# A two-block transformer kernel on one core: expert gates made by one-hot products in PSUM, or scattered into a DRAM table

## The reference, cut to what matters

```python
def peer(xn, peer_w_q, peer_sub_keys, peer_u, peer_v):
    qh = (xt @ peer_w_q).reshape(T, PEER_HEADS, 2, PEER_HALF)
    sub = jnp.einsum("thpc,hpnc->thpn", qh, peer_sub_keys)
    v1, i1 = lax.top_k(sub[:, :, 0], PEER_TOPK)      # 16 of 128
    v2, i2 = lax.top_k(sub[:, :, 1], PEER_TOPK)
    vals, cidx = lax.top_k(v1[..., :, None] + v2[..., None, :], PEER_TOPK)
    experts = e1 * N_KEYS + e2
    gates = jax.nn.softmax(vals, axis=-1)
    # y[token] = sum over its 128 (head, k): gelu(x . u[expert]) * gate * v[expert]
```

## Time and profile before

| | |
|---|---|
| three runs | 3204.29, 3204.08, 3206.46 us |
| profiled execution | span 3203.0 us |
| TensorE matmul busy | 3185.0 us, 99% |
| VectorE busy | 2226.0 us, 69% |
| ScalarE busy | 1555.5 us, 49% |
| GpSimd busy | 13.7 us, 0% |
| DMA | 610.61 MB, 191 GB/s; SyncE's queue 60.0% of 16 engines |
| granted TensorE clock | 0.9 or more in every slice |

### The profile page before, as it was taken

The page is one execution under the profiler, slowest core; times in us unless marked ns, Lnnn a source line. Parts: engine busy times, 40 slices in busy tenths (PEclk is TensorE's granted clock), DMA queues, the critical chain, the costliest instruction groups (busy, mean ns, idle before and its releaser), DMA issues.

```text
span 3203.0 us, 42378 instructions
## 1 busy us (share of the span) xinstructions
PE 3185.0 (99%) x17362; PEld 2707.6 (85%) x17362; DVE 2226.0 (69%) x3055; ACT 1555.5 (49%) x1998; POOL 13.7 (0%) x29
## 2 busy tenths in 40 slices
PE   9999999999999999999999999999999999999999
PEld 8888888888888888887888888888888788888887
DVE  6775556677577567766568997766687787865564
ACT  4564444555355455546544555455443344444353
POOL 0000000000000000000000000000000000000000
PEclk9999999999999999999999999999999999999999
DMA  7456665656665666653555666666666665556665
GB/s 252 154 162 218 211 211 180 210 191 191 191 190 190 193 188 192 205 170 111 190 154 171 217 216 189 188 183 224 190 190 212 203 200 173 188 184 192 194 184 171
DMA packets 175825, 610.61 MB, mean 191 GB/s; under 512 B 19201, under 2 KB 27553, under 8 KB 174736
## 3 DMA queue, kind: packets, MB, share of 16 engines
q1 hardware_dynamic: 173648, 599.93, 60.0%
q0 software_dynamic: 1984, 7.99, 0.8%
HBM read 597.36 MB, written 10.49 MB: 190 GB/s over the span
## 4 chain that ended last, share of the span: by engine, by line
PE 97%; DVE 2%; ACT 1%; issue 0%; DMA 0%; SPq 0%; ACTq 0%; DVEq 0%
PE PS L1194 29%; PE PS L1211 16%; PE PS L1213 16%; PE PS L1212 16%; PE PS L1191 15%; PE PS L1414 1%; PE PS L1427 1%; PE PS L1293 1%; DVE LO L1749 0%; PE PS L1247 0%; PE PS L1326 0%; ACT UN L1506 0%; ACT HI L1436 0%; PE PS L1305 0%; PE PS L1223 0%
## 5 line engine op out<-in xcount | busy, mean ns | idle before, releaser
L1749 DVE TENSOR_TENSOR LO<-RAW,HI 128x1024 fp32r<-128x1024 f32 (+1 forms) x1096 | 1325.1, 1218 | 698.0 <-ACT HI L1436 694.7
L1436 ACT ACTIVATE HI<-RAW 128x1024 fp32r<-128x1024 f32 (+1 forms) x1096 | 1148.3, 1054 | 1044.6 <-PE PS L1213 732.5
L1194 PE MATMUL PS<-XX,HI 128*128 128x512 f32 x4032 | 968.4, 391 | 0.0
L1194 PEld LDWEIGHTS PS<-XX,HI 128*128 128x128 f32 x4032 | 739.4, 188 | 145.1 <-issue 2.4
L1211 PE MATMUL PS<-HI,FH 128*128 128x512 f32 x1760 | 692.0, 393 | 1.7 <-DVE LO L1749 1.7
L1213 PE MATMUL PS<-HI,FL 128*128 128x512 f32 x1760 | 685.8, 390 | 0.0
L1212 PE MATMUL PS<-LO,FH 128*128 128x512 f32 x1760 | 684.7, 389 | 0.0
L1191 PEld LDWEIGHTS PS<-XX,LO 128*128 128x128 f32 x4032 | 520.2, 191 | 21.1 <-issue 1.0
L1191 PE MATMUL PS<-XX,LO 128*128 128x256 f32 x4032 | 536.8, 284 | 0.0
L1213 PEld LDWEIGHTS PS<-HI,FL 128*128 128x128 f32 x1760 | 330.3, 188 | 70.1
L1211 PEld LDWEIGHTS PS<-HI,FH 128*128 128x128 f32 x1760 | 330.3, 188 | 69.1 <-DVE LO L1749 2.2
(11 more groups left out here) (286 smaller groups left out, 1667.7 us busy)
## 6 DMA issues: line engine op xcount, KB each, us to landing
RAW<-in_peer_ut SPq DMA_DIRECT2D x256, 512.0 KB, 4.1
RAW<-in_peer_v SPq DMA_DIRECT2D x256, 512.0 KB, 4.2
RAW<-in_ffn_w_up SPq DMA_DIRECT2D x176, 512.0 KB, 4.2
RAW<-in_w_in SPq DMA_DIRECT2D x88, 512.0 KB, 4.3
RAW<-in_ffn_w_down SPq DMA_DIRECT2D x88, 512.0 KB, 4.2
RAW<-in_w_in_c SPq DMA_DIRECT2D x48, 512.0 KB, 3.7
RAW<-in_w_mix_out SPq DMA_DIRECT2D x32, 512.0 KB, 4.0
RAW<-in_w_in_2c SPq DMA_DIRECT2D x32, 512.0 KB, 3.7
```

The lines of the kernel that those rows point to most:

```text
L1194: m = e.matmul(o, hi[:, k, x], XX[:, 4 * u + k, :, :].rearrange("p h s -> p (h s)"), start=first and k == 0, stop=last and k == 3, skip_gr ...
L1436: return e.activation(dst, src, ACT.Copy) if scale is None else e.activation(dst, src, ACT.Copy, scale=scale)
L1749: return e.tensor_tensor(dst, src, hi.bitcast(F32), ALU.subtract)
```

## The change

`gates` becomes a DRAM table of 16384 experts by 256 tokens (16 MB). It is zeroed by 32 DMAs of 512 KB, DRAM to DRAM, issued by SyncE one after each of the first 32 products of the feed-forward up stage of the first block. Each `choose(t, g)` gets a tenth part after one more yield: VectorE computes the table address of each of its 32 gates per token (`address`, two instructions), and GpSimd issues 32 indirect DMAs (`scatter`), each of which adds one float for each of 128 tokens into the table. Before each head's 16 DMAs GpSimd waits until all earlier ones of the same token half have landed, since two heads can name the same expert. There are 256 in all. `gates_in(c, j)` then loads 512 KB of the table, on GpSimd's queue too: those of chunks 1 and 0 right behind the last scatter, the others when their place in SBUF is free. Tables, one-hots, `gates_sum`, `gates_out`, `gates_side`, the DRAM copies and chunks 3 and 4 set aside all go; only chunks 0, 1, 2 are staged (in GM[2], STAGE, UF), and chunks 3 to 7 go up and down in turn. `rate[0]` stays at 0.68 through the three up stages.

```diff
-    order = [("up", c) for c in (3, 4, 0, 1, 2)] + [("down", c) for c in (1, 0, 2, 3, 4)]
-    order += [(d, c) for c in range(5, 8) for d in ("up", "down")]
+    order = [("up", c) for c in range(3)] + [("down", c) for c in (1, 0, 2)]
+    order += [(d, c) for c in range(3, 8) for d in ("up", "down")]
...
                     product(("f", q, i, b), 4)
+                    if zeroed[0] < ZEROS:
+                        emit("zero", zeroed[0])
+                        zeroed[0] += 1
...
         emit("gate", t, g)
+        yield
+        emit("address", t, g)
+        emit("scatter", t, g)
...
+    def first_gates():
+        for c in (1, 0):
+            for j in range(4):
+                emit("gates_in", c, j)
+        yield
+
     background.extend([first_gates(), first_blocks()])
-    for c in (3, 4, 0, 1, 2):
+    for c in range(3):
         up_staged(c)
...
-    background.extend([gates_back(2), multiply_third()])
+    gates_in(2)
+    background.append(multiply_third())
     down(1, then=0)
-    background.append(gates(2, 3))
+    gates_in(4)
     down(0, then=2)
-    beside.append(gates_back(3))
-    down(2, then=3)
-    down(3, then=4)
-    background.extend([pause(4), gates(3, 3)])
-    down(4)
-    for c in range(5, 8):
+    gates_in(5)
+    down(2)
+    gates_in(3)
+    for c in range(3, 8):
+        if c in (4, 5):
+            gates_in(c + 2)
...
+            elif kind == "zero":
+                n, = k
+                e.dma_start(GATES[:, 1024 * n:1024 * n + 1024], a["zeros"]).then_inc(l_zero, 16)
...
+            elif kind == "scatter":
+                t, g = k
+                w.wait_ge(l_zero, 16 * ZEROS)
+                w.wait_ge(s_dve, V("address", t, g))
+                for h in (2 * g, 2 * g + 1):
+                    if h:
+                        w.wait_ge(l_scatter[t], 256 * h)
+                    for i in range(16 * h, 16 * h + 16):
+                        e.indirect_dma_start(a["gates"], bass.IndirectOffsetOnAxis(IDX[:, t, i:i + 1], 0),
+                                             TK[:, t, i:i + 1], None, compute_op=ALU.add).then_inc(l_scatter[t], 16)
+            elif kind == "gates_in":
+                c, j = k
+                if c < 2:
+                    for t in range(2):
+                        w.wait_ge(l_scatter[t], 256 * 8)
+                else:
+                    w.wait_ge(s_dve, {2: V("second_mul", 3), 3: V("split_up", 2, 3), 4: V("third_mul", 3),
+                                      5: V("split_up", 0, 3), 6: V("weigh", 3, 3), 7: V("weigh", 4, 3)}[c])
+                e.dma_start(GM[PLACE[c]][:, 4 * j:4 * j + 4, :].rearrange("p c s -> p (c s)"),
+                            GATES[:, 4096 * c + 1024 * j:4096 * c + 1024 * j + 1024]).then_inc(l_gates[PLACE[c]][j], 16)
...
             elif kind == "first_mul":
                 j, = k
                 w.wait_ge(s_act, A("us_gelu", 0, j))
-                w.wait_ge(s_act, A("gates_out", 31))
+                w.wait_ge(*gates_landed(0, j))
```

More of the change, by code:

```diff
@@ L22 @@
 LOOK = 3
+NKEY = 128
+ZEROS = 32
 CONSTS = {}
@@ L128 @@
     "best": (0, 0, 5), "cand0": (0, 0, 8), "cand1": (0, 0, 6), "pick0": (0, 0, 7), "pick1": (0, 1, 6),
-    "gate": (0, 0, 3), "tables": (2, 0, 13),
-    "onehot": (0, 0, 3), "gates_sum": (1, 0, 0), "gates_out": (0, 3, 0), "gates_side": (1, 0, 2),
-    "us": (0, 1, 1), "us_gelu": (0, 1, 0), "split_aside": (0, 1, 2), "first_mul": (0, 1, 1), "second_mul": (0, 1, 2), "third_mul": (0, 0, 1), "split_up": (0, 1, 1),
+    "gate": (0, 0, 3), "address": (0, 0, 2),
+    "us": (0, 1, 1), "us_gelu": (0, 1, 0), "first_mul": (0, 1, 1), "second_mul": (0, 1, 2), "third_mul": (0, 0, 1), "split_up": (0, 1, 1),
     "x": (0, 1, 1), "gelu": (0, 2, 0), "weigh": (0, 1, 2), "y": (0, 0, 2),
@@ L652, in plan @@
         background.extend(choose(t, g) for t in range(2))
[L654 to L694, removed]
     staged = [[] for _ in range(5)]
@@ L740, in from_chip @@
             yield from pause(2)
[L742 to L749, removed]
     def down(c, then=None):
@@ L753, in down @@
             if g == 3 and then is not None:
-                beside.append((from_aside if then > 2 else from_chip)(then))
+                beside.append(from_chip(then))
             product(("y", c, g), 8)
@@ L760, in plan, with gates_in @@
     rate[0] = 1
-    background.extend([gates_back(2), multiply_third()])
+    def gates_in(c):
+        for j in range(4):
+            emit("gates_in", c, j)
+    gates_in(2)
+    background.append(multiply_third())
     down(1, then=0)
-    background.append(gates(2, 3))
+    gates_in(4)
     down(0, then=2)
-    beside.append(gates_back(3))
-    down(2, then=3)
-    down(3, then=4)
-    background.extend([pause(4), gates(3, 3)])
-    down(4)
-    for c in range(5, 8):
+    gates_in(5)
[4 more added lines that the diff above has]
+            gates_in(c + 2)
         for j in range(4):
@@ L886, in _program @@
     HB = over("HB", [128, 4, S], 32 * K)
[L887 to L895, removed]
+    IDX = at("IDX", [128, 2, NKEY], U32, offset=gb_at + 4 * K)
     BP = at("BP", [128, 2, S], offset=const_at + 4 * CONSTS["mask2"][0])
-    TAB = at("TAB", [128, 2, S], BF16, offset=mask1_at)
-    KEYS2 = at("KEYS2", [128, 128, 2], BF16, offset=mask1_at + K)
     PS = ctx.enter_context(nc.psum_tensor("PS", [128, 4096], F32))
@@ L992, in _program @@
     l_raw = [sem(f"l_raw{i}") for i in range(NRAW)]
[L993 to L996, removed]
+    l_zero = sem("l_zero")
+    l_scatter = [sem(f"l_scatter{t}") for t in range(2)]
+    l_gates = [[sem(f"l_gates{i}_{j}") for j in range(4)] for i in range(3)]
     l_x, l_ident, l_const, l_par, l_small, l_gb, l_gb1, l_bi, l_gb2, l_keys, l_out = [sem("l_" + n) for n in (
@@ L1022, in multiplied, with gates_landed @@
         return (LAST[step] if u is None else FIRST[step] + u) + 1
-    def gates_read(r, blk):
-        return P("gates_side", r, blk) if r else P("gates_sum", blk)
+    GATES_BY_PLACE = {0: (0, 3, 6), 1: (1, 2, 4, 7), 2: (5,)}
+    def gates_landed(c, j):
+        return l_gates[PLACE[c]][j], 16 * GATES_BY_PLACE[PLACE[c]].index(c) + 16
+    GATES = a["gates"].rearrange("(p x) o -> p (x o)", p=128)
     FFN_ENDS = ("res1", 3), ("d", 0, 3), ("d", 1, 3)
@@ L1395, in tensor @@
                     m.then_inc(s_pe, 1)
[L1396 to L1416, removed]
-            elif kind == "gates_side":
-                r, blk = k
-                i = blk % 2
-                w.wait_ge(s_dve, V("onehot", r, blk))
-                for half in range(2):
-                    for s, n in until_free(step, half):
-                        w.wait_ge(s, n)
-                b0 = 2048 + 512 * PLAN.bank[step, 0]
-                for j in range(8):
-                    o = PS[:, b0 + 128 * j:b0 + 128 * j + 96].rearrange("p (i s) -> p i s", i=3)
-                    m = e.matmul(o, OH2[:, i, j // 2, :, j % 2], GOH[:, i, j // 2, :, :, j % 2], start=True,
-                                 stop=True, skip_group_check=True)
-                m.then_inc(s_pe, 1)
     @block.scalar
@@ L1696, in scalar @@
                 e.activation(dd, dd, ACT.Exp).then_inc(s_act, 1)
-            elif kind == "gates_out":
-                blk, = k
-                w.wait_ge(s_pe, P("n2_turn", 3))
-                w.wait_ge(s_dve, V("gate", 1, 3))
-                w.wait_ge(s_pe, P("gates_sum", blk))
-                src = spare(("gates_sum", blk)).rearrange("p (s k) -> p k s", k=64)
-                for i in range(2):
-                    copy(GM[i][:, :, 8 * blk:8 * blk + 8], src[:, 16 * i:16 * i + 16]).then_inc(s_act, 1)
-                if blk >= 2:
-                    w.wait_ge(l_pass[blk % 2], 16 * (blk // 2))
-                copy(PASS[:, blk % 2].rearrange("p i (k s) -> p (i k) s", s=8), src[:, 32:64]).then_inc(s_act, 1)
             elif kind == "us_gelu":
@@ L1726, in scalar @@
                 copy(blocks(FH, j), blocks(GM[2] if c == 0 else GM[0], j)).then_inc(s_act, 1)
-            elif kind == "split_aside":
-                c, j = k
-                w.wait_ge(s_mm, multiplied(("y", c - 1, 3), 2 * j + 1))
-                w.wait_ge(s_dve, V(*step, k=1))
-                copy(blocks(FH, j), HB[:]).then_inc(s_act, 1)
             elif kind == "gelu":
@@ L2063, in vector @@
                 w.wait_ge(s_act, A(*step))
-                w.wait_ge(s_dve, V("weigh", c, j - 1) if j else V("weigh", c - 1, 3) if c > 5 else V("split_aside", 4, 3))
+                w.wait_ge(s_dve, V("weigh", c, j - 1) if j else V("weigh", c - 1, 3) if c > 3 else V("second_mul", 3))
                 e.tensor_tensor(HB[:, 2 * k[2]:2 * k[2] + 2, :], halves(step)[:, :, 0, :], BP[:],
@@ new lines, in vector @@
+            elif kind == "address":
+                t, g = k
+                first, second = (TK[:, t, 128 * n + 32 * g:128 * n + 32 * g + 32] for n in (1, 2))
+                w.wait_ge(l_const, 16)
+                w.wait_ge(s_dve, V("gate", t, g))
```

(11 more changed lines are left out.)

88 lines of the change are left out of this document (8 added, 80 removed).

## The result

The changed kernel takes **3415.17 us** (3414.29 to 3416.14) against 3204.49 us before: a ratio of 1.0658, 95% interval 1.0643 to 1.0673. That is 211 us slower, and outside the range that was given (3167 to 3310).

What follows compares the result with a forecast made beforehand. TensorE, busy for 99% of the span, was taken to bound the kernel. A 58 us gain less a 39 us stall gave 3204.3 - 19 = 3185 us, likeliest 3175 to 3196, 8 in 10 from 3167 to 3310.

Steps and rivals of the forecast that it cites:

- What goes and what moves: TensorE's first and side passes go, 60 us; two chunks moved to the up-and-down part lose 2: 58 us gain.
- The cheap parts: Zeroing DMAs, address instructions on VectorE and gates_in loads for chunks 2 to 7, all taken as hidden: 0 us.
- Spacing of the groups: Time between successive groups of 32 indirect DMAs while choose runs: 37.6 us.
- The last address: VectorE computes it at unit 82 of the 96 staged ones; first_mul follows 4.1 us later.
- The landings: GpSimd's wait in the middle of a group and the landing of the last indirect DMAs: 4.0 us each.
- The formula: TensorE's stall at first_mul: S = P + 7 x max(0, P - 37.6) + 3.3 us, giving 39 us.
- P: GpSimd's time for one group of 32 indirect DMAs, 32c plus the wait in its middle: 36 us.
- S: TensorE's stall at first_mul while the gates go through GpSimd, DRAM and back: 39 us.
- c: GpSimd's time for one indirect DMA in the scatter: 1.0 us, bounded by 0.51 to 0.56 below and 4.5 above.
- Rival A: GpSimd cannot keep pace with groups 37.6 us apart: slower past c = 1.12 us, 3302 us at 1.5; chance 0.25.
- Rival C: VectorE holds GpSimd up during the scatter: c is 1.6 us, S = 182 us, 3328 us; chance 0.08.
- Rival D: The scatter's adds drain slowly, sharing 16 queues with 512 KB weight loads: 3328 us or more; chance 0.08.

Runs made afterwards that it cites:

- the half scatter: Against the changed kernel, leaves out the gates of every second head, 128 indirect DMAs in place of 256: 3186.6 us.
- the added transfers: Against the changed kernel, adds 80 DRAM-to-DRAM transfers of 512 KB by SyncE while VectorE waits at first_mul: 3502.9 us.

## Why the prediction was wrong, step by step

- *What goes and what moves* (60 less 2, so 58 us): 57.6 us by the kernel without a scatter; 3203.0 - (3414.1 - 264.6) = 53.5 us by the changed kernel's own trace, and 56 if the 2.5 us of low clock behind the stall are taken off too. Right to within some 3 us, about what single runs can tell.
- *The cheap parts* at 0: right. 252 units in 700 us in the zeroing stretch in both kernels, and 82 units in 230 us of the `choose` stretch in both.
- *Spacing of the groups*, 37.6 us: measured 37.8. *The last address*, then `first_mul` at once: right.
- *The landings*, 4.0 us each: 12.8/4 = 3.2 us beside weight traffic, 7.1/4 = 1.8 in the stall. The fixed cost of about 2.0 us that the Trainium skill gives in "DMA: Bandwidth & Descriptors", section "Anatomy of one DMA — SWDGE (gpsimd) path", is nearer the second, once the DMA engines were quiet; small either way.
- *The formula*: with P = 65.1, S = 65.1 + 7 x 27.5 + 3.3 = 261 us; TensorE's stall measured 263. Right, and confirmed at 37 us by the half scatter. Two numbers taken from it were worked out wrongly, and neither moves the forecast: at c = 4.5 it gives 924 us and not 1050, and at c = 1.07 a time of 3192 us and not 3196.
- **The step that failed: "To it I add as much again, rounded down, for fetching 128 indices and for the add: c = 1.0 us."** It measured 1.96: 0.96 for an indirect store, 0.58 more for the add, 0.12 on the mean for VectorE, 0.30 between two. The nearest row was a direct DMA, another kind of instruction, and the 0.30 between instructions had no row, since direct DMAs went out without a gap. As the formula has a slope of 256 us per us of c past 1.05, the error of 0.96 was worth 234 us; shorter waits in the middle of the groups gave back 12, which leaves the 222 between 39 and 261. Rival A named this, with its threshold at 1.12, but its price stopped at c = 1.5, and so did the range. An upper bound of 4.5 us was written down and then not used: a term multiplied by 256 with ends at 0.54 and 4.5 could not be given a range that closed at 1.5.
- Rival C (VectorE holds GpSimd up) is a real effect of 0.12 us on the mean, worth some 30 us of the 211, and not the cause. Rival D (the queues drain slowly) was not seen in the changed kernel, where no wait for a landing was over 4.2 us; under the traffic of the added transfers it was, with 90 us.

## What to carry to other kernels

Here work that was handed to a slow serial queue cost nothing until the moment that an in-order engine asked for it, and then all of its backlog at once: compute the queue's pace, compare it with the arrivals, and count the stall at the first consumer. The remedy can be the consumer's place as well as the queue's speed: here four chunks of other products ahead of it turned 3415 into 3150 us without touching the scatter. Where one unmeasured price is multiplied by hundreds and sits near a threshold, the range belongs to its bounds, not to the favourite.

## What the runs showed of the hardware that was not expected

- An adding indirect DMA of 128 single floats holds GpSimd for 1.54 us, a storing one for 0.96 us, a direct one for 0.54 us, plus 0.30 us between indirect ones; 64 indices instead of 128 save 0.13 us.
- While single floats were stored into DRAM, TensorE stood up to 2.2 us between two matmuls of one product, and 52 units went through in 230 us; while they were added, 82 did. The cause is open.
- VectorE instructions with two SBUF inputs lengthened an indirect DMA from 1.54 to 1.88 us; 323 GB/s of other traffic did not lengthen it.
- Sixteen adds of 128 floats took 90 us to land beside a queue of 80 transfers of 512 KB on another engine's queue.
- TensorE's clock fell to its lower level, 1.2 GHz, while it stood idle, and came back only after it had worked again. Stretches of the changed kernel, columns as in the earlier trace rows:

```profile
1975.00:2221.00 246.00, 1.08 (x9) 0.88 (x7) 0.00 (x0) 0.00 (x0) 200.51 (x131) 0.51 0.22 0
...
2237.00:2241.00 4.00, 2.21 (x9) 2.21 (x10) 3.49 (x3) 1.42 (x2) 0.00 (x0) 0.50 0.32 89
2241.00:2245.00 4.00, 4.00 (x13) 3.10 (x12) 2.88 (x4) 2.01 (x2) 0.00 (x0) 0.66 0.51 182
2245.00:2250.00 5.00, 5.00 (x32) 4.42 (x31) 2.93 (x4) 3.88 (x5) 0.00 (x0) 1.00 0.35 112
```

The granted share is 0.50 until 2241, 0.66 in the next 4 us and 1.00 from 2245. If it was at half rate from 2238.8 to 2243.7, which gives the mean of 0.66, that is a cost of about 2.5 us (an estimate), which the formula did not hold.
